# One core, two transformer blocks in fp32: chunk 0 of a chunked scan moved ahead of and between the steps of a pooling projection

## The chip, the core and the metric

The program runs on one core of a Trainium2 chip. The metric is the device time of one launch in microseconds (us), the median of three runs. Five engines work side by side and meet at semaphores: PE (TensorE, matmuls), DVE (VectorE), ACT (ScalarE), POOL (GpSimd), and SP (SyncE), which here only issues DMAs.

## What is computed

`reference()` runs two transformer blocks over 512 tokens of width 1024, batch 1. The change lies in the first block's hybrid mixer. Cut to that:

```python
proj = u @ w_in                                   # z, xbc, dt_raw, v
y = ssd_chunked(xs, dt, a, bm, cm)                # 4 chunks of 128 tokens, 16 heads of 64
y = y + d_skip[:, None] * xs
y = y.reshape(bsz, s, SSD_INNER) * silu(z)
y_ssd = rmsnorm(y, ssd_norm)
y_pool = multi_scale_pool(v, pool_w, pool_scale)  # 4 groups, a 256x256 product each, times pool_scale
return concatenate([y_ssd, y_pool]) @ w_out
```

Inside `ssd_chunked`, for a chunk c: `y_diag = (cb * seg) @ x`, where `seg = exp(a_cs[l] - a_cs[s])` below the diagonal; `states = b^T (decay * x)`; the running state is `prev[c+1] = exp(a_cs_end) * prev[c] + states[c]`; `y_off = (c @ prev[c]) * exp(a_cs)`. Chunk 0 has no `y_off`.

## The kernel before

Every fp32 product of this stretch is made of three matmuls over operands split into a high and a low part (`w_hi`/`w_lo`, `x_hi`/`x_lo`, `y_hi`/`y_lo`). Weights come in jobs of 256 columns: SP loads a job into `w_raw`, POOL splits it (`w_hi` in one instruction, `w_lo` in four) as soon as the job that last used the same half of `w_hi`/`w_lo` is through, which PE signals by `w_used`. PE writes job results into pairs of `g_bank`, everything small into the four `t_bank` banks, which are taken in turn by the position of a task in the table `TASKS`; PE waits on `t_free` of a bank until its last user has been read out. The order of instructions on each engine is written out by hand, one block per engine, and each engine works strictly in that order.

The stretch that the change touches follows the z projection. PE: `state(0)` (the state of chunk 0), the job `pool` (four groups of 12 matmuls, `products_T` with `kt=2`; two pairs of banks in turn, so group g waits for `yp_lo` of group g-2), `inside(0)` (y_diag of chunk 0, 32 small matmuls), then for each chunk c: `state(c)`, `from_state(c)` (y_off), `inside(c)`, and the job `wo_pool + c` of 48 matmuls, a quarter of the pooled half of the output projection. Between two of its 16 steps of three matmuls (`turned`), PE transposes the finished 128 tokens of the scan (task `yT{c}`, two banks).

A chunk's way over the other engines: DVE copies or adds the state (L2848, L2850), multiplies d_skip by xs (L2864), adds y_diag (L2869), multiplies by silu(z) (L2877, signals `y_ready`); ACT takes the sum of squares and the root (L2088, L2089); DVE prepares the next chunk's `xdt` (L2802) and state (L2886), takes the reciprocal (L2888, `yr_ready`); ACT scales `y_nat` (L1854, `yn_ready`); PE transposes (L1329); ACT writes `x_hi` from the banks (L1854) and DVE `x_lo` (L2899), which frees the banks. `decay(c)` on ACT turns the broadcast log decays of chunk c into `seg`: 16 instructions (L2058, "shifts", one per head) and one exponential (L2061, `seg_ready`); DVE multiplies them by the scores (L2814, `scores_decayed`, `m_ready`), in its order ahead of the x_lo of the chunk before. For the pooling ACT evicts `y_hi` (two instructions a group) and DVE `y_lo` (L2824).

The tasks of the table around chunk 0 stand in this order: state0, ydiag0, yT0, state1, yoff1, ydiag1, two banks each. SP sends the broadcast of chunk 2's decays (L651) once ydiag0 is done, and the weights of `wo_pool + 2` behind it. By the table yoff1 uses the two banks of yT0, and PE's `from_state(1)` waits until DVE has written the last `x_lo` of chunk 0. PE's own order is shown by `from_state`:

```python
pe.wait_ge(prev_ready, c)
for g in range(GROUPS):
    b = bank(TASKS[f"yoff{c}"] + g)      # waits for t_free of that bank
    nc.tensor.matmul(b, cT[...], state_into(c, g, g + 1), start=True, stop=True)
```

Of the kernel before, what the change touches and what calls it, by code (L numbers as in the profile page):

```python
# [231 lines left out]
def program(nc, A, out):  # L232
    with ExitStack() as ctx:
# [1618 lines left out]
        def _(act):  # L1852
# [224 lines left out]
            for g in range(4):  # L2077
                act.wait_ge(pool_group, g + 1)
                for f in range(2):
                    copy(y_hi[:, 2 * g + f, :], g_bank[:, 2 * ((j + 1 + g) % 2) + f, :], col["pool_scale"](2 * g + f)).then_inc(yp_hi, 1)  # L2080
            for c in range(CHUNKS):

                if c < CHUNKS - 1:
                    decay(c + 1)
# [534 lines left out]
        def _(dve):  # L2619
# [219 lines left out]
            for c in range(CHUNKS):  # L2839
                xv = xs_nat(c).rearrange("p (h d) -> p h d", h=HEADS)  # L2840
                halves = [slice(g * HPG, (g + 1) * HPG) for g in range(2)]
                if c < CHUNKS - 1:
                    for g in range(2):
                        r = TASKS[f"state{c}"] + g
                        b = ready(r).rearrange("p (k i d) -> p k i d", i=2, d=HD)
                        into = state_into(c + 1, g, g + 1)
                        if c == 0:
                            ins = v.tensor_copy(into, b)  # L2848
                        else:
                            ins = v.tensor_tensor(into, into, b, ALU.add)  # L2850
                        if g == 0:
                            ins.then_inc(t_free[BANK[r]], 1)
                        else:
                            done(ins, t_free[BANK[r]], prev_ready)
# [8 lines left out]

                link(v.tensor_tensor(xdd[:], xv, bc[:, 2, :].unsqueeze(2).to_broadcast([P, HEADS, HD]), ALU.mult))  # L2864
                for g in range(2):
                    r = TASKS[f"ydiag{c}"] + g
                    b = ready(r).rearrange("p (h d) -> p h d", h=HPG)
                    other = y_nat if c else xdd
                    ins = v.tensor_tensor(y_nat[:, halves[g], :], other[:, halves[g], :], b, ALU.add)  # L2869
                    if g == 0:  # L2870
                        ins.then_inc(t_free[BANK[r]], 1)
                    else:
                        done(ins, t_free[BANK[r]])
                if c:
                    link(v.tensor_tensor(y_nat[:], y_nat[:], xdd[:], ALU.add))
                dve.wait_ge(zs_ready, 4)
                v.tensor_tensor(y_nat[:], y_nat[:], zs[:, c, :].rearrange("p (h d) -> p h d", h=HEADS), ALU.mult).then_inc(y_ready, 1)  # L2877
# [668 lines left out]
```

## Time and profile before

| | |
|---|---|
| median of three runs | 1652.65 us (1652.22 to 1652.96) |
| the profiled execution | 1652.55 us, span 1650.8 us |
| PE busy | 1627.0 us, 99% of the span |
| DVE, ACT, POOL busy | 1046.3, 664.6, 1039.3 us |
| PE's granted clock, mean | 0.999 of full speed |

The span runs from the first to the last instruction of the profiled execution. The stretch that the change touches lies at 238 to 325 us of it.

### The profile page before, as it was taken

How to read it: one execution, taken by the hardware profiler on the slowest of the kernel's cores; microseconds unless marked ns; L12 is line 12 of the kernel's file. 1: busy time of each engine (PE TensorE's matmuls, PEld its weight loads, DVE VectorE, ACT ScalarE, POOL GpSimd, SP SyncE). 2: the span in 40 equal slices, each digit the busy share in tenths (PEclk: the TensorE clock that was granted, in tenths of full speed). 3: DMA queues.
4: the chain of work that ended last, by engine and by line, in shares of the span. 5: the costliest groups of instructions: out<-in, count | busy, mean ns of one | idle time of the engine just before them, and what ended most of it. 6: DMA issues, size and time to landing. Idle time of an engine off the chain costs nothing.

```text
span 1650.8 us, 23774 instructions
## 1 busy us (share of the span) xinstructions
PE 1627.0 (99%) x8755; PEld 1381.9 (84%) x8755; DVE 1046.3 (63%) x1634; ACT 664.6 (40%) x1166; POOL 1039.3 (63%) x788
## 2 busy tenths in 40 slices
PE   6999999999999999999999999999999999999998
PEld 5898897888978999999988888887878778877887
DVE  5323948773537745745757997999656786556624
ACT  5422237420324523623544446765312245555301
POOL 7676764566647784784765888784467643334664
PEclk9999999999999999999999999999999999999999
DMA  6333333322243242342334323222233222111231
GB/s 212 118 114 104 128 103 105 100 94 90 98 153 102 77 129 76 103 128 78 102 103 128 91 88 102 77 77 77 93 137 110 77 77 77 52 51 52 77 115 64
DMA packets 188347, 162.59 MB, mean 98 GB/s; under 512 B 7636, under 2 KB 184400, under 8 KB 187728
## 3 DMA queue, kind: packets, MB, share of 16 engines
q1 hardware_dynamic: 188040, 161.10, 30.7%
q8 instruction: 67, 1.10, 0.3%
q14 instruction: 40, 0.33, 0.1%
q10 hardware_dynamic: 200, 0.06, 0.0%
HBM read 155.87 MB, written 4.23 MB: 97 GB/s over the span
## 4 chain that ended last, share of the span: by engine, by line
PE 93%; DVE 4%; ACT 1%; DMA 1%; issue 1%; POOL 0%; DVEq 0%; SPq 0%; ACTq 0%
PE g_bank L1046 54%; PE g_bank L1420 10%; PE g_bank L1080 6%; PE g_bank L1070 5%; PE g_bank L1483 2%; PE t_bank L1420 2%; PE t_bank L1759 2%; PE g_bank L1629 1%; PE t_bank L1771 1%; PE t_bank L1371 1%; PE t_bank L1403 1%; PE t_bank L1748 1%; PE t_bank L1547 1%; PE t_bank L1568 1%; PE g_bank L1611 1%; PE t_bank L1304 1%
## 5 line engine op out<-in xcount | busy, mean ns | idle before, releaser
L803 POOL TENSOR_SCALAR w_hi<-w_raw 128x2048 fp32r<-128x2048 f32 x67 | 132.6, 1979 | 387.3 <-PE g_bank L1046 160.9
L820 POOL TENSOR_TENSOR w_lo<-w_raw,w_hi 128x512 fp32r<-128x512 f32 x264 | 367.0, 1421 | 5.5
L1046 PE MATMUL g_bank<-x_hi,w_hi 128*128 128x512 f32 x912 | 364.5, 400 | 0.4 <-DVEq L2633 0.4
L1046 PE MATMUL g_bank<-x_hi,w_lo 128*128 128x512 f32 x912 | 355.4, 390 | 0.0
L1046 PE MATMUL g_bank<-x_lo,w_hi 128*128 128x512 f32 x912 | 355.2, 389 | 0.0
L1046 PEld LDWEIGHTS g_bank<-x_hi,w_hi 128*128 128x128 f32 x912 | 171.3, 188 | 38.9 <-issue 4.8
L1046 PEld LDWEIGHTS g_bank<-x_hi,w_lo 128*128 128x128 f32 x912 | 171.2, 188 | 36.1
L1046 PEld LDWEIGHTS g_bank<-x_lo,w_hi 128*128 128x128 f32 x912 | 171.4, 188 | 35.2 <-issue 1.4
L3175 DVE SCALAR_TENSOR_TENSOR t_bank<-hc,cols,t_bank 128x512 f32<-128x512 f32 x280 | 187.0, 749 | 4.9 <-DVE hc L3159 3.0
L954 POOL TENSOR_TENSOR w_lo<-w_raw,w_hi 128x512 fp32r<-128x512 f32 x100 | 127.3, 1305 | 67.7 <-ACT w_hi L2279 67.7
L1046 PE MATMUL g_bank<-y_hi,w_hi 128*128 128x512 f32 x288 | 113.5, 394 | 0.0
L1046 PE MATMUL g_bank<-y_hi,w_lo 128*128 128x512 f32 x288 | 112.2, 390 | 0.0
L1046 PE MATMUL g_bank<-y_lo,w_hi 128*128 128x512 f32 x288 | 112.1, 389 | 0.0
L899 POOL TENSOR_TENSOR w_lo<-w_raw,w_hi 128x512 fp32r<-128x512 f32 x57 | 73.0, 1295 | 39.6 <-ACT w_hi L1854 39.6
L972 POOL TENSOR_TENSOR pacc<-pacc,prod 128x512 f32<-128x512 f32 x54 | 68.1, 1292 | 0.0
L1420 PE MATMUL g_bank<-x_lo,w_hi 128*128 128x256 f32 x228 | 64.5, 283 | 0.0
L1420 PE MATMUL g_bank<-x_hi,w_lo 128*128 128x256 f32 x228 | 64.5, 283 | 0.0
L1420 PE MATMUL g_bank<-xt_hi,w_hi 128*128 128x256 f32 x228 | 64.5, 283 | 0.0
L1420 PE MATMUL g_bank<-xt_lo,w_hi 128*128 128x256 f32 x228 | 64.5, 283 | 0.0
L1420 PE MATMUL g_bank<-xt_hi,w_lo 128*128 128x256 f32 x228 | 64.5, 283 | 0.0
L1420 PE MATMUL g_bank<-x_hi,w_hi 128*128 128x256 f32 x228 | 64.5, 283 | 0.0
L1046 PEld LDWEIGHTS g_bank<-y_hi,w_hi 128*128 128x128 f32 x288 | 54.1, 188 | 11.9 <-issue 0.7
(565 smaller groups left out, 3983.5 us busy)
## 6 DMA issues: line engine op xcount, KB each, us to landing
w_raw<-w_gate_up SPq DMA_DIRECT2D x44, 512.0 KB, 4.8
w_raw<-a_w_in SPq DMA_DIRECT2D x44, 512.0 KB, 4.4
w_raw<-b_w_in SPq DMA_DIRECT2D x38, 512.0 KB, 4.3
w_raw<-w_in SPq DMA_DIRECT2D x28, 512.0 KB, 4.5
w_raw<-w_kv SPq DMA_DIRECT2D x16, 512.0 KB, 4.3
w_raw<-w_out_mix SPq DMA_DIRECT2D x16, 512.0 KB, 6.3
w_raw<-w_down SPq DMA_DIRECT2D x16, 512.0 KB, 4.4
w_raw<-a_w_out SPq DMA_DIRECT2D x16, 512.0 KB, 4.3
```

The costliest lines, as they stand in the source:

```text
L803: nc.gpsimd.tensor_scalar(w_hi[:, par], w_raw[:, par], 1.0, 0.0, ALU.mult, ALU.add).then_inc(pool_chain, 1)
L820: last = nc.gpsimd.tensor_tensor(w_lo[:, par, s], w_raw[:, par, s], w_hi[:, par, s].bitcast(F32), ALU.subtract)
L899: return nc.gpsimd.tensor_tensor(lo, src, hi.bitcast(F32), ALU.subtract)
L954: last = nc.gpsimd.tensor_tensor(lo[:, s], w_raw[:, j % 2, s], hi[:, s].bitcast(F32), ALU.subtract)
L972: nc.gpsimd.tensor_tensor(acc_k[:], acc_k[:], p[:], ALU.add).then_inc(tap_chain, 1)
L1046: last = nc.tensor.matmul(g_bank[:, 2 * pair + f if banks is None else banks[f], 0:n], ww[:, k0 + k, ws], xk, start=(k == 0 and q == 0), s ...
L1070: last = nc.tensor.matmul(g_bank[:, 2 * par + f, :], ww[:, par, k, ws], xx[:, k0 + k, :], start=(k == 0 and q == 0), stop=(k == kt - 1 and ...
L1080: last = nc.tensor.matmul(g_bank[:, 2 * par + m // 2, m % 2 * WC:m % 2 * WC + n], xx[:, k, m * P:(m + 1) * P], ww[:, k, 0:n], start=(k == ...
L1420: last = nc.tensor.matmul(out, ww[:, k, :], xx[:, k, :], start=(k == 0 and q == 0), stop=(k == HK - 1 and q == 2))
L1483: last = nc.tensor.matmul(g_bank[:, DOWN_BANKS[c][0][f], :], ww[:, k, ws], xx[:, k, :], start=(k == 0 and q == 0), stop=(k == n - 1 and q ...
L1759: last = nc.tensor.matmul(b[:, c:c + W_OF[qb]], qB[:, 4 * hg + i, qb * P:(qb + 1) * P], kB[:, 0:W_OF[qb]], start=True, stop=True)
L3175: ins = v.scalar_tensor_tensor(tail if k == TAPS - 1 else a(k), h(k), wk, a(k), ALU.mult, ALU.add)
```

## The change

On PE, `inside(0)` is done right behind `state(0)`, ahead of the pooling's products. The last pooling group signals `w_used` itself, and the wait for all of `yp_lo` that stood between pooling and `wo_pool` is spread over steps 0, 6 and 7 of job `wo_pool`. The transposes of chunk 0 come after step 12 of that job and not after step 14. On DVE, the state, sums and d_skip product of chunk 0 stand ahead of the pooling's evictions, and the gate of chunk 0 between the second and the third of them. On ACT, the 16 shifts of chunk 1 are split: five behind the second pooling group, five behind the third, six with the exponential behind the scaling of chunk 0's `y_nat`, ahead of its `x_hi`. `add_state`, `add_inside` and `gated_by_z` are the old statements made into functions.

```diff
@@ -1306,6 +1306,7 @@
 
             j = JOBS["pool"]
             state(0)
+            inside(0)
             slot(j, j % 2, j // 2)
             for g in range(4):
                 if g == 0:
@@ -1314,12 +1315,12 @@
                     pe.wait_ge(yp_lo, 2 * g - 2)
                 pe.wait_ge(d_lo, 2 * g + 2)
                 last = products_T(j % 2, y_hi, y_lo, kt=2, k0=2 * g, x0=2 * g, pair=(j + 1 + g) % 2)
-                last.then_inc(pool_group, 1)
+                last.then_inc(pool_group if g < 3 else w_used, 1)
 
             def turned(c):
 
                 def turn(step):
-                    if step == (14 if c == 0 else 12):
+                    if step == 12:
                         pe.wait_ge(yn_ready, c + 1)
                         yv = y_nat[:].rearrange("p h d -> p (h d)")
                         for g in range(2):
@@ -1330,16 +1331,18 @@
                             last.then_inc(t_ready, 1)
                 return turn
 
-            inside(0)
-            pe.wait_ge(yp_lo, 8)
-            pe.nop().then_inc(w_used, 1)
+            def pool_rests(step):
+
+                if step in (0, 6, 7):
+                    pe.wait_ge(yp_lo, max(step, 5) + 1)
+
             for c in range(CHUNKS):
                 if c:
                     state(c)
                     from_state(c)
                     inside(c)
 
-                jobs(JOBS["wo_pool"] + c, 1, lambda par: products_T(par, y_hi, y_lo, between=turned(c)))
+                jobs(JOBS["wo_pool"] + c, 1, lambda par: products_T(par, y_hi, y_lo, between=turned(c), before=None if c else pool_rests))
             products_as_ready(JOBS["wo_ssd"], x_hi, x_lo, lambda k: pe.wait_ge(ys_lo, 8 * (CHUNKS - 1) + k + 1))
             pe.wait_ge(mem2_n, MT)
             for i in range(4):
@@ -2051,12 +2054,14 @@
             d_split(2)
             raw_pair(JOBS["v"] + 3)
 
-            def decay(c):
+            def decay(c, h0=0, h1=HEADS):
                 act.wait_ge(in_abc[c], 32)
-                for h in range(HEADS):
+                for h in range(h0, h1):
                     d = decay_of(c, h)
                     ins = nc.scalar.activation(d, d, ACT.Relu, bias=acs[:, c, h:h + 1], scale=-1.0)
                     ins.then_inc(relu_d, 1)
+                if h1 < HEADS:
+                    return
                 act.wait_ge(relu_d, HEADS * (c + 1))
                 nc.scalar.activation(decays(c), decays(c), ACT.Exp, scale=-1.0).then_inc(seg_ready, 1)
 
@@ -2075,12 +2080,17 @@
                 act.nop().then_inc(zs_ready, 1)
             j = JOBS["pool"]
             for g in range(4):
-                act.wait_ge(pool_group, g + 1)
+                if g < 3:
+                    act.wait_ge(pool_group, g + 1)
+                else:
+                    act.wait_ge(w_used, j + 1)
                 for f in range(2):
                     copy(y_hi[:, 2 * g + f, :], g_bank[:, 2 * ((j + 1 + g) % 2) + f, :], col["pool_scale"](2 * g + f)).then_inc(yp_hi, 1)
+                if g in (1, 2):
+                    decay(1, 5 * (g - 1), 5 * g)
             for c in range(CHUNKS):
 
-                if c < CHUNKS - 1:
+                if 0 < c < CHUNKS - 1:
                     decay(c + 1)
                 if c:
                     link(nc.scalar.activation(ysum[:, c, 1:2], eps[:, 0:1], ACT.Sqrt))
@@ -2089,6 +2099,8 @@
                 nc.scalar.activation(ysum[:, c, 1:2], ysum[:, c, 0:1], ACT.Sqrt, bias=eps[:, 0:1], scale=1.0 / SSD_INNER).then_inc(ysq_ready, 1)
                 act.wait_ge(yr_ready, c + 1)
                 copy(y_nat[:], y_nat[:], ysum[:, c, 0:1]).then_inc(yn_ready, 1)
+                if c == 0:
+                    decay(1, 10)
                 for g in range(2):
                     b = ready(TASKS[f"yT{c}"] + g)
...
+            def add_state(c):
+
+                for g in range(2):
+                    r = TASKS[f"state{c}"] + g
...
@@ -2873,8 +2862,48 @@
                         done(ins, t_free[BANK[r]])
                 if c:
                     link(v.tensor_tensor(y_nat[:], y_nat[:], xdd[:], ALU.add))
+
+            def gated_by_z(c):
+
                 dve.wait_ge(zs_ready, 4)
                 v.tensor_tensor(y_nat[:], y_nat[:], zs[:, c, :].rearrange("p (h d) -> p h d", h=HEADS), ALU.mult).then_inc(y_ready, 1)
+
+            add_state(0)
+            add_inside(0)
+            j = JOBS["pool"]
+            for k in range(8):
+
+                if k == 2:
+                    gated_by_z(0)
+                dve.wait_ge(yp_hi, k + 1)
+                ins = v.scalar_tensor_tensor(y_lo[:, k, :], g_bank[:, 2 * ((j + 1 + k // 2) % 2) + k % 2, :], col["pool_scale"](k),
+                                             y_hi[:, k, :].bitcast(F32), ALU.mult, ALU.subtract)
+                done(ins, yp_lo, *([g_free[j % 2]] * (k == 7)))
+            def add_projection(c):
+
+                j = JOBS["wo_pool"] + c
+                dve.wait_ge(w_used, j + 1)
+                for f in range(2):
+                    k = 2 * c + f
+                    ins = v.tensor_tensor(hT[:, k, :], hT[:, k, :], g_bank[:, 2 * (j % 2) + f, :], ALU.add)
+                    if f == 0:
...
```

PE from `state(0)` to the transposes of chunk 0, before (L1286 is state, L1046 the jobs' products, L1304 y_diag, L1329 the transposes; the names behind "waits" are the semaphores; "..." stands for more rows of L1046):

```order
L1286 MATMUL t_bank<-xdd,b_nat 128x512 [waits t_free2,xdt_ready]
L1286 MATMUL t_bank<-xdd,b_nat 128x512 [waits t_free3]
L1046 MATMUL g_bank<-y_hi,w_hi 128x512 [waits g_free0,d_lo,g_free1,w_split]
...
L1046 MATMUL g_bank<-y_hi,w_hi 128x512 [waits d_lo,yp_lo]
...
L1304 MATMUL t_bank<-xdt,m__99 128x64 [waits t_free0,m_ready]
L1304 MATMUL t_bank<-xdt,m__99 128x64 x7
L1304 MATMUL t_bank<-xdt,m__99 128x64 [waits t_free1]
L1304 MATMUL t_bank<-xdt,m__99 128x64 x7
L1046 MATMUL g_bank<-y_hi,w_hi 128x512 [waits yp_lo,g_free0,w_split]
...
L1329 MATMUL t_bank<-ident,y_nat 128x128 [waits t_free2,yn_ready]
```

and in the changed kernel (the transposes are L1330 there):

```order
L1286 MATMUL t_bank<-xdd,b_nat 128x512 [waits t_free2,xdt_ready]
L1286 MATMUL t_bank<-xdd,b_nat 128x512 [waits t_free3]
L1304 MATMUL t_bank<-xdt,m__99 128x64 [waits t_free0,m_ready]
L1304 MATMUL t_bank<-xdt,m__99 128x64 x7
L1304 MATMUL t_bank<-xdt,m__99 128x64 [waits t_free1]
L1304 MATMUL t_bank<-xdt,m__99 128x64 x7
L1046 MATMUL g_bank<-y_hi,w_hi 128x512 [waits g_free0,d_lo,g_free1,w_split]
...
L1046 MATMUL g_bank<-y_hi,w_hi 128x512 [waits d_lo,yp_lo]
...
L1046 MATMUL g_bank<-y_hi,w_hi 128x512 [waits yp_lo,g_free0,w_split]
...
L1046 MATMUL g_bank<-y_hi,w_hi 128x512 [waits yp_lo]
...
L1046 MATMUL g_bank<-y_hi,w_hi 128x512 [waits yp_lo]
...
L1330 MATMUL t_bank<-ident,y_nat 128x128 [waits t_free2,yn_ready]
```

y_diag of chunk 0 has moved up past the 48 matmuls of the pooling, three waits for `yp_lo` stand inside the job behind it, and the transposes stand two steps earlier in that job.

ACT from the second pooling group to the first `x_hi` of chunk 0, before (`m_xl` holds the decays of chunk 1, L1854 is a copy):

```order
L1854 ACTIVATE y_hi<-g_bank,cols 128x512 [waits pool_group]
L1854 ACTIVATE y_hi<-g_bank,cols 128x512
L2058 ACTIVATE m_xl<-m_xl,acs 128x128 [waits in_abc1]
L2058 ACTIVATE m_xl<-m_xl,acs 128x128 x15
L2061 ACT_TABLE_LOAD
L2061 ACTIVATE m_xl<-m_xl 128x8x256 [waits relu_d]
L2088 ACTIVATE xdd,ysum<-y_nat 128x1024 [waits y_ready]
L2089 ACT_TABLE_LOAD
L2089 ACTIVATE ysum<-ysum,eps 128x1 [waits act_chain]
L1854 ACTIVATE y_nat<-y_nat,ysum 128x1024 [waits yr_ready]
L1854 ACTIVATE x_hi<-t_bank,cols 128x128 [waits t_ready]
```

and in the changed kernel (L1857 is the copy, L2061 the shifts, L2066 the exponential):

```order
L2061 ACTIVATE m_xl<-m_xl,acs 128x128 [waits in_abc1]
L2061 ACTIVATE m_xl<-m_xl,acs 128x128 x4
...
L2061 ACTIVATE m_xl<-m_xl,acs 128x128 [waits in_abc1]
L2061 ACTIVATE m_xl<-m_xl,acs 128x128 x4
...
L2099 ACTIVATE ysum<-ysum,eps 128x1 [waits act_chain]
L1857 ACTIVATE y_nat<-y_nat,ysum 128x1024 [waits yr_ready]
L2061 ACTIVATE m_xl<-m_xl,acs 128x128 [waits in_abc1]
L2061 ACTIVATE m_xl<-m_xl,acs 128x128 x5
L2066 ACT_TABLE_LOAD
L2066 ACTIVATE m_xl<-m_xl 128x8x256 [waits relu_d]
L1857 ACTIVATE x_hi<-t_bank,cols 128x128 [waits t_ready]
```

The shifts of chunk 1 are split in three, and the last six of them, a table load and the exponential now stand between the scaling of `y_nat` and the first `x_hi`.

## Rows read from the trace of the kernel before

**Rows 1.** Page, part 1: busy us, share of the span, instructions.

```profile
PE 1627.0 (99%) x8755; PEld 1381.9 (84%) x8755; DVE 1046.3 (63%) x1634; ACT 664.6 (40%) x1166; POOL 1039.3 (63%) x788
```

**Rows 2.** Waits of PE, 220 to 330 us: total, times, longest.

```profile
PE t_bank L1329 <- ACT y_nat L1854: 1.3, 1, 1.3
```

**Rows 3.** Timeline of PE, chunk 0: start, duration, instruction, count [idle before].

```profile
240.40 0.53 PE L1046 MATMUL g_bank<-y_hi,w_hi 128*128 128x512 f32 x1
...
251.59 3.68 PE L1304 MATMUL t_bank<-xdt,m__99 128*128 128x64 f32 x32
255.07 0.48 PE L1046 MATMUL g_bank<-y_hi,w_hi 128*128 128x512 f32 x1
...
266.87 1.09 PE L1329 MATMUL t_bank<-ident,y_nat 128*128 128x128 f32 x8 [1.30 <-ACT y_nat L1854]
...
268.49 1.88 PE L1286 MATMUL t_bank<-xdd,b_nat 128*128 128x512 f32 x4
...
271.70 0.70 PE L1294 MATMUL t_bank<-prev,cT 128*128 128x512 f32 x1 [0.25 <-DVEq L2633]
```

**Rows 4.** Timeline of PE, chunk 1 and the start of chunk 2.

```profile
272.66 3.68 PE L1304 MATMUL t_bank<-xdt,m_xl 128*128 128x64 f32 x32
276.15 0.48 PE L1046 MATMUL g_bank<-y_hi,w_hi 128*128 128x512 f32 x1
...
285.10 1.03 PE L1329 MATMUL t_bank<-ident,y_nat 128*128 128x128 f32 x8
...
288.05 1.88 PE L1286 MATMUL t_bank<-xdd,b_nat 128*128 128x512 f32 x4
289.76 1.88 PE L1294 MATMUL t_bank<-prev_x,cT 128*128 128x512 f32 x4
```

**Rows 5.** Timeline of DVE, pooling to the end of chunk 0.

```profile
244.22 0.75 DVE L2824 SCALAR_TENSOR_TENSOR y_lo<-g_bank,cols,y_hi 128x512 fp32r<-128x512 f32 x1 [18.23 <-ACT y_hi L1854]
...
252.50 1.65 DVE L2824 SCALAR_TENSOR_TENSOR y_lo<-g_bank,cols,y_hi 128x512 fp32r<-128x512 f32 x2 [1.07 <-ACT y_hi L1854]
...
260.88 2.32 DVE L2802 TENSOR_TENSOR xdt<-xs,dt__105 128x1024 f32<-128x1024 f32 x1
263.12 2.31 DVE L2886 TENSOR_TENSOR prev_x<-prev,cdec 128x1024 f32<-128x1024 f32 x1
...
266.67 2.35 DVE L2814 TENSOR_TENSOR m_xl<-m_xl,cbm 128x1024 f32<-128x1024 f32 x2
...
270.37 1.12 DVE L2899 SCALAR_TENSOR_TENSOR x_lo<-t_bank,cols,x_hi 128x128 fp32r<-128x128 f32 x4 [0.31 <-PE t_bank L1286]
```

**Rows 6.** Instructions on tile y_nat, the gate's: ns min/median/max, starts.

```profile
L2877 DVE TENSOR_TENSOR y_nat<-y_nat,zs x4: 1226/1226/2021, 258.9 to 316.3; 128x1024 f32<-128x1024 f32 x4
```

**Rows 7.** Timeline of ACT, chunk 0.

```profile
251.78 1.26 ACT L1854 ACTIVATE y_hi<-g_bank,cols 128x512 fp32r<-128x512 f32 x2 [1.45 <-PE g_bank L1046]
...
265.66 1.15 ACT L1854 ACTIVATE y_nat<-y_nat,ysum 128x1024 f32<-128x1024 f32 x1 [1.91 <-DVE ysum L2888]
...
269.57 4.80 ACT L2058 ACTIVATE m__99<-m__99,acs 128x128 f32<-128x128 f32 x16
274.39 1.28 ACT L2061 ACT_TABLE_LOAD   x1
275.68 1.92 ACT L2061 ACTIVATE m__99<-m__99 128x2048 f32<-128x2048 f32 x1
```

**Rows 8.** Timeline of POOL, the splits of two weight tiles.

```profile
254.49 1.91 POOL L803 TENSOR_SCALAR w_hi<-w_raw 128x2048 fp32r<-128x2048 f32 x1 [8.29 <-PEq L1335]
256.48 7.86 POOL L820 TENSOR_TENSOR w_lo<-w_raw,w_hi 128x512 fp32r<-128x512 f32 x4
268.85 1.92 POOL L803 TENSOR_SCALAR w_hi<-w_raw 128x2048 fp32r<-128x2048 f32 x1 [4.51 <-PE g_bank L1046]
```

**Rows 9.** Timeline of PE at the start, behind an idle stretch.

```profile
12.79 3.67 PE L1139 MATMUL t_bank<-ident,xn_nat 128*128 128x128 f32 x16 [2.35 <-ACT xn_nat L1854]
```

**Rows 10.** The same stretch by windows: busy us (instructions) of each engine, PE's granted clock.

```profile
12.79:16.46 3.67, 3.67 (x17) 3.67 (x18) 1.38 (x2) 2.16 (x4) 3.50 (x5) 1.00 1.05 382
```

More of the change, by code:

```diff
@@ L2819, in _, with add_inside @@
             scores_decayed(0)
+            def add_state(c):
+                for g in range(2):
+                    r = TASKS[f"state{c}"] + g
+                    b = ready(r).rearrange("p (k i d) -> p k i d", i=2, d=HD)
+                    into = state_into(c + 1, g, g + 1)
+                    if c == 0:
+                        ins = v.tensor_copy(into, b)
+                    else:
+                        ins = v.tensor_tensor(into, into, b, ALU.add)
+                    if g == 0:
+                        ins.then_inc(t_free[BANK[r]], 1)
+                    else:
+                        done(ins, t_free[BANK[r]], prev_ready)
+            halves = [slice(g * HPG, (g + 1) * HPG) for g in range(2)]
+            def add_inside(c):
+                xv = xs_nat(c).rearrange("p (h d) -> p h d", h=HEADS)
+                link(v.tensor_tensor(xdd[:], xv, bc[:, 2, :].unsqueeze(2).to_broadcast([P, HEADS, HD]), ALU.mult))
+                for g in range(2):
+                    r = TASKS[f"ydiag{c}"] + g
+                    b = ready(r).rearrange("p (h d) -> p h d", h=HPG)
+                    other = y_nat if c else xdd
+                    ins = v.tensor_tensor(y_nat[:, halves[g], :], other[:, halves[g], :], b, ALU.add)
+                    if g == 0:
+                        ins.then_inc(t_free[BANK[r]], 1)
+                    else:
+                        done(ins, t_free[BANK[r]])
+                if c:
+                    link(v.tensor_tensor(y_nat[:], y_nat[:], xdd[:], ALU.add))
+            def gated_by_z(c):
+                dve.wait_ge(zs_ready, 4)
+                v.tensor_tensor(y_nat[:], y_nat[:], zs[:, c, :].rearrange("p (h d) -> p h d", h=HEADS), ALU.mult).then_inc(y_ready, 1)
+            add_state(0)
+            add_inside(0)
             j = JOBS["pool"]
             for k in range(8):
+                if k == 2:
+                    gated_by_z(0)
                 dve.wait_ge(yp_hi, k + 1)
@@ L2839, in _ @@
             for c in range(CHUNKS):
[L2840 to L2854, printed above, removed]
+                if 0 < c < CHUNKS - 1:
+                    add_state(c)
                 if c:
@@ L2862, in _ @@
                                         ALU.mult).then_inc(t_free[BANK[r]], 1)
[L2864 to L2877, printed above, removed]
+                    add_inside(c)
+                    gated_by_z(c)
                 if c < CHUNKS - 1:
```

## Prediction, before the changed kernel was run

> **What bounds the kernel now.** The page comes first: PE is busy for 99% of the span [rows 1], so nearly everything added to PE's path lengthens the run, and nothing can be gained but PE's waits. The view of waits, narrowed to the stretch of the change, says how much that is: one wait of 1.3 us, for ACT's scaling of y_nat ahead of the transposes of chunk 0 [rows 2]. PE's timeline shows the second, smaller one: the second y_off of chunk 1 starts at 271.70 behind an idle 0.25 us, released by DVE [rows 3]; in chunk 2 the state and y_off follow each other 1.71 us apart, with no wait [rows 4]. The reader should then look at the other engines' timelines not for busy shares but for what ends when: DVE finishes the last x_lo of chunk 0 at 271.49 [rows 5], and PE goes on 0.21 us later [rows 3]. That pair of banks is the joint between the chunks. All times below are of the profiled execution (1652.55 us, its span 1650.8); it lies 0.1 us under the median of the runs, so a difference found in it is simply added to the median.
>
> **y_diag ahead of the pooling.** The 32 small matmuls take 3.48 us before (251.59 to 255.07) and the four pooling groups 11.19 us (240.40 to 251.59), 2.80 us each [rows 3]. Exchanged, y_diag runs from 240.40 to 243.9, and the groups end at 246.7, 249.5, 252.3 and 255.1. Their sum is the same, so this costs nothing by itself. The work that DVE gains before the first eviction lies in 18.2 us in which it is idle today [rows 5]. The gate does not: it lands between the second and the third eviction. The first eviction starts 1.0 us behind its group's end (244.22 against 240.40 + 2.80), a pair takes 1.65 us [rows 5], and the gate takes 1.23 us where nothing disturbs it, 2.02 us where POOL splits beside it [rows 6]. Four evictions and the gate end at 246.7 + 1.0 + 1.65 + 0.2 + 1.23 + 1.65 = 252.4 us; the fourth group needs them at 252.3. That is a new wait of 0.15 us (0.9 us at 2.02). I take 0.15, since POOL's earlier split should be through by then. Job wo_pool 0 starts at 255.25 instead of 255.07. On SP the broadcast of chunk 2's decays waits for y_diag of chunk 0, and a weight load stands behind it; both can now go some 11 us earlier (255.07 to 243.9), and since nobody waits for them sooner, and POOL still splits by `w_used`, this is nothing either way. The waits at its steps 0, 6 and 7 ask for evictions that trail each group by as much as today, 2.56 us behind the last (254.15 against 251.59) [rows 3, 5], and step 6 is over 4 us into the job: nothing.
>
> **Shifts among the evictions.** Sixteen take 4.80 us, 0.30 each [rows 7]. ACT's eviction of a group ends 1.45 us behind the group (253.04 against 251.59), five shifts take 1.5 us, in all 2.95 us, against 2.80 + 0.20 us to the next eviction: they just fit. Cost nothing, at most 0.1.
>
> **Transposes at step 12.** In chunk 1 they come 8.95 us into the job (276.15 to 285.10) [rows 4], so PE wants them at 264.2. DVE ends its last eviction at 255.25 + 2.56 = 257.8, starts xdt 0.24 later, needs 4.55 us for xdt and the state (260.88 to 265.43), and 1.44 us later PE can go on (266.87) [rows 3, 5]: 264.0. In time. The whole job then takes the 11.90 us of chunk 1 (276.15 to 288.05) [rows 4] and ends at 267.15, 1.34 us before today's 268.49. This is the gain that the change can hold, up to here.
>
> **What now stands ahead of x_hi.** ACT ends the scaling at 264.0, and then come six shifts (1.8), the table load (1.28) and the exponential (1.92) [rows 7]: 269.0. Before, all of this lay ahead of the y_ready of chunk 0, in a stretch in which ACT had nothing else to do. Two things queue behind it: x_hi on ACT, and on DVE, which goes in order, the scores of chunk 1, and behind these x_lo, which frees the banks of yT0. PE is done with state 1 at 267.15 + 1.71 = 268.85 [rows 4] and stands before y_off.
>
> The scores took 2.35 us undisturbed (266.67 to 269.02), ahead of POOL's next split [rows 5, 8]. Now they meet it. POOL starts 0.36 us behind the end of the job (268.85 against 268.49) [rows 3, 8], so at 267.5, and its first instruction runs for 1.9 us, to 269.4. What such a meeting costs is shown by xdt and the state: 2.3 us each under the split of 256.48 against 1.2 us for a score instruction of the same size [rows 5, 8]; that is, they take turns, 1.15 us each. So: first scores from 269.4 to 270.6, POOL to 271.75, second scores to 272.9. From there to the last x_lo it is 2.47 us as before (269.02 to 271.49), x_hi being written beside the scores: 275.35, and PE's second y_off at 275.55 (+0.21) instead of 271.70. Behind it, order and durations are those of before on every engine, PE has no wait there that could swallow the delay, and DVE's chain for chunk 1 is delayed by the same amount. **Sum: +3.85 us**, 1656.5 us. All gains of the part before (1.34 us) are in it.
>
> What the notes say of such a load would make it worse. Before the exponential the load takes 1.28 us, and the exponential starts within 0.02 us of its end (274.39 + 1.28 against 275.68) [rows 7]. The Trainium skill (ScalarE: Activation LUTs, What ACT_TABLE_LOAD costs) puts a drain of about 1.38 us beside each load, 2.66 us in all. By that the scores would start at about 270.4 and the sum be about +5; the trace shows no such drain, and the sum goes by the trace.
>
> **The rivals.**
> A, the forecast: +3.85. Its own spread is the waits sized above, the order in which DVE and POOL meet, and a turn lost or won (1.15): 1655.7 to 1657.6.
> B, PE loses its rate as well. It would stand idle from about 269.2 to 274.05 (x_lo of the first bank, 272.9 + 1.12 + a hand-over), far longer than any wait before [rows 2]. The only stretch behind an idle time of this length is the program's start: there 16 transposes take 3.67 us, against 1.03 us for eight in chunk 1 [rows 4, 9], 1.6 us more, though the granted clock reads 1.00, which is 2.4 GHz [rows 10]. For it: the slow start. Against it: that clock column, and that the first transposes may have waited for ACT. Price: 1.6 to 2.5 us on top of A, 1658.1 to 1659.0. The Trainium skill (TensorE: Matmul & The Clock Gate, Why this matters for your kernels) says that a TensorE left idle between bursts of matmuls falls to half clock, which speaks for B; these rows neither show such a fall nor exclude it.
> C, DVE and POOL do not take turns over the scores (they hit POOL's first instruction, which is of another kind than those of 256.48): 269.05 + 2.35 + 2.47 + 0.21 = 274.1, +2.4, 1655.0. Not distinguishable from before.
> D, not slower: the split of 255.6 does not hold up xdt and the state, so each takes 1.2 instead of 2.3 us. y_nat is scaled 2.2 us earlier, the exponential ends at 266.8, before POOL starts, the scores end at 269.15 and y_off comes at 271.85: +0.15, 1652.8. It decides from the point where the scores end before 272.3 us (then the delay is under 3.3 us). Against it: this split begins at the end of the pooling today as well, and xdt and the state lie under it [rows 5, 8].
>
> **How the numbers follow.** 0.2% is 3.3 us, about what a measurement of this kernel tells from no change. A has 0.50, B 0.30, C 0.14, D 0.06. Most of A (0.42) and all of B lie over 1655.95: slower 0.72. The rest of A, C and most of D are within 0.2%: 0.26. Faster would take more than 3.3 us of gain where PE's waits hold about 2 us: 0.02. The range takes in A, C and nearly all of B, 1654.8 to 1658.9; A alone is 1655.7 to 1657.6.
>
> **What the profile of the changed kernel would show.** Right: no idle time of PE ahead of the transposes of chunk 0; state 1 at about 267.2; then PE idle for about 5 us ahead of the first y_off of chunk 1, put down to DVE, and 0.6 us ahead of the second; the exponential of chunk 1 at about 267; the two score instructions together near 3.8 us; y_diag of chunk 1 at about 276.5 instead of 272.66. For B: matmul durations doubled behind the wait, or a granted clock of 0.5. Wrong: x_hi written before the exponential (then I misread ACT's order), a wait at the third or fourth pooling group of over a microsecond, or a wait later in the kernel that shrinks by as much as this one grows.

## The result, and the profile after

The changed kernel takes 1659.81 us (median of five runs, 1657.61 to 1662.10), against 1652.65 us (1651.52 to 1652.96) before: a ratio of 1.0047, 95% interval 1.0036 to 1.0058, 7.2 us longer. The prediction had 1656.5 us and a range up to 1658.9. One of the five executions, at 1657.61 us, lies within that range; its mean granted clock is 0.998, that of the others 0.994 or 0.995. Of the experiments below, e3 and e4 had one execution each at a mean clock of 0.85 and 0.57 (1806 and 2674 us), which is left out of every figure here.

The profiled execution took 1660.07 us, its span is 1658.4 us. Everything up to the state of chunk 0 is the same program in both kernels, yet it starts at 237.02 us here and at 238.82 us in the profile of before; over the profiles of this study it varies from 236.8 to 239.0 us. So I give places as times behind that start, S, in what follows. The view of waits of PE, 235 to 330 us, has one line:

```profile
PE t_bank L1294 <- DVEq L2645: 5.0, 1, 5.0
```

The 1.3 us of [rows 2] are gone, and 5.0 us ahead of the first y_off of chunk 1 have come, more than there was to win. PE's timeline:

```profile
237.02 1.88 PE L1286 MATMUL t_bank<-xdd,b_nat 128*128 128x512 f32 x4
...
250.69 0.50 PE L1046 MATMUL g_bank<-y_hi,w_hi 128*128 128x512 f32 x1
...
262.41 1.03 PE L1330 MATMUL t_bank<-ident,y_nat 128*128 128x128 f32 x8
...
265.34 1.88 PE L1286 MATMUL t_bank<-xdd,b_nat 128*128 128x512 f32 x4
272.20 3.75 PE L1294 MATMUL t_bank<-prev,cT 128*128 128x512 f32 x4 [4.99 <-DVEq L2645]
275.75 6.93 PE L1304 MATMUL t_bank<-xdt,m_xl 128*128 128x64 f32 x32
282.44 0.77 PE L1046 MATMUL g_bank<-y_hi,w_hi 128*128 128x512 f32 x1
283.01 0.63 PE L1046 MATMUL g_bank<-y_lo,w_hi 128*128 128x512 f32 x1
...
295.65 1.88 PE L1286 MATMUL t_bank<-xdd,b_nat 128*128 128x512 f32 x4
```

Against [rows 3, 4]: the transposes come at S+25.39 without a wait, the state of chunk 1 at S+28.32 instead of S+29.67, y_off at S+35.18. But look at the durations behind the wait: y_diag, 32 matmuls, takes 6.93 us and not 3.68, and the first products of the next job start 0.43 us apart, not 0.23. From y_diag on (S+38.73 instead of S+33.84, +4.89) the delay grows to +8.09 at the start of job wo_pool 1 (282.44, S+45.42 instead of S+37.33) and +9.40 at the state of chunk 2 (S+58.63 instead of S+49.23). The windows say why (busy us of PE, PEld, DVE, ACT, POOL with their instructions, granted clock, share of the DMA engines, GB/s):

```profile
268.00:270.00 2.00, 0.00 (x0) 0.00 (x0) 2.00 (x2) 2.00 (x9) 2.00 (x2) 1.00 0.00 0
270.00:272.00 2.00, 0.00 (x0) 0.00 (x0) 1.91 (x5) 2.00 (x9) 2.00 (x2) 0.88 0.00 0
272.00:274.00 2.00, 1.80 (x2) 0.79 (x3) 1.54 (x5) 1.97 (x7) 2.00 (x2) 0.50 0.00 0
278.00:280.00 2.00, 2.00 (x11) 2.00 (x11) 1.76 (x2) 0.00 (x0) 0.00 (x0) 0.50 0.03 8
284.00:286.00 2.00, 2.00 (x8) 1.57 (x7) 1.97 (x3) 0.00 (x0) 0.00 (x0) 0.71 0.00 0
```

The granted clock falls to 0.50, 1.2 GHz, late in PE's idle stretch (0.88 over 270 to 272 is full clock up to about 271.5) and is back at 1.00, 2.4 GHz, at about 285.2 (0.71 over 284 to 286): 13.6 us at half clock. Such times of a fall are worked out from the share of a window that was spent at each of the two levels. The 9.4 us of this stretch, less the 1.8 us by which this execution reached it sooner, are the 7.6 us between the spans.

DVE, ACT and POOL in the same stretch, one view each:

```profile
247.79 1.22 DVE L2869 TENSOR_TENSOR y_nat<-y_nat,zs 128x1024 f32<-128x1024 f32 x1
...
256.36 1.92 DVE L2814 TENSOR_TENSOR xdt<-xs,dt__105 128x1024 f32<-128x1024 f32 x1 [0.24 <-DVE y_lo L2879]
258.19 2.31 DVE L2915 TENSOR_TENSOR prev_x<-prev,cdec 128x1024 f32<-128x1024 f32 x1
...
266.90 3.97 DVE L2826 TENSOR_TENSOR m_xl<-m_xl,cbm 128x1024 f32<-128x1024 f32 x2 [4.17 <-ACT m_xl L2066]
...
272.22 1.12 DVE L2928 SCALAR_TENSOR_TENSOR x_lo<-t_bank,cols,x_hi 128x128 fp32r<-128x128 f32 x4 [0.31 <-DVE x_lo L2928]
```

```profile
260.73 1.15 ACT L1857 ACTIVATE y_nat<-y_nat,ysum 128x1024 f32<-128x1024 f32 x1 [3.08 <-DVE ysum L2917]
261.79 1.85 ACT L2061 ACTIVATE m_xl<-m_xl,acs 128x128 f32<-128x128 f32 x6
263.66 1.28 ACT L2066 ACT_TABLE_LOAD   x1
264.95 1.91 ACT L2066 ACTIVATE m_xl<-m_xl 128x2048 f32<-128x2048 f32 x1
266.77 2.15 ACT L1857 ACTIVATE x_hi<-t_bank,cols 128x128 fp32r<-128x128 f32 x8
```

```profile
265.70 1.90 POOL L803 TENSOR_SCALAR w_hi<-w_raw 128x2048 fp32r<-128x2048 f32 x1 [1.82 <-PE g_bank L1046]
267.68 6.78 POOL L820 TENSOR_TENSOR w_lo<-w_raw,w_hi 128x512 fp32r<-128x512 f32 x4
```

ACT has the scaling of y_nat done at 261.9, and only at 266.8 begins with x_hi; the exponential lies between. DVE waits 4.17 us for it, then takes 3.97 us for the two score instructions, which took 2.35 us [rows 5], because POOL's split lies beside them, and the last x_lo ends at 273.34.

### The profile page after: what moved, and what is told of

It is laid out like the page before. It is cut to its first block, busy times and chain, and to the rows that moved or that the text cites. A ratio compares the mean times of both kernels' runs of the same rounds, so it can differ in the third digit from the quotient of the medians.

```text
span 1658.4 us, 23772 instructions
## 1 busy us (share of the span) xinstructions
PE 1632.3 (98%) x8755; PEld 1386.9 (84%) x8755; DVE 1047.3 (63%) x1634; ACT 663.0 (40%) x1165; POOL 1041.2 (63%) x788
## 4 chain that ended last, share of the span: by engine, by line
PE 93%; DVE 4%; ACT 2%; issue 1%; DMA 1%; POOL 0%; DVEq 0%; SPq 0%; ACTq 0%
PE g_bank L1046 53%; PE g_bank L1423 10%; PE g_bank L1080 6%; PE g_bank L1070 5%; PE g_bank L1486 2%; PE t_bank L1423 2%; PE t_bank L1762 2%; PE g_bank L1632 1%; PE t_bank L1774 1%; PE t_bank L1304 1%; PE t_bank L1374 1%; PE t_bank L1406 1%; PE t_bank L1751 1%; PE t_bank L1550 1%; PE t_bank L1571 1%; PE g_bank L1220 1%
## 5 line engine op out<-in xcount | busy, mean ns | idle before, releaser
L1046 PE MATMUL g_bank<-x_hi,w_hi 128*128 128x512 f32 x912 | 364.5, 400 | 0.3 <-DVEq L2645 0.2
L1046 PE MATMUL g_bank<-x_hi,w_lo 128*128 128x512 f32 x912 | 355.4, 390 | 0.0
L1046 PE MATMUL g_bank<-x_lo,w_hi 128*128 128x512 f32 x912 | 355.2, 390 | 0.0
L1046 PEld LDWEIGHTS g_bank<-x_hi,w_hi 128*128 128x128 f32 x912 | 171.3, 188 | 38.7 <-issue 4.8
L1046 PEld LDWEIGHTS g_bank<-x_hi,w_lo 128*128 128x128 f32 x912 | 171.2, 188 | 36.2
L1046 PEld LDWEIGHTS g_bank<-x_lo,w_hi 128*128 128x128 f32 x912 | 171.5, 188 | 35.1 <-issue 1.4
L1046 PE MATMUL g_bank<-y_hi,w_hi 128*128 128x512 f32 x288 | 114.0, 396 | 0.0
L1046 PE MATMUL g_bank<-y_hi,w_lo 128*128 128x512 f32 x288 | 112.7, 391 | 0.0
L1046 PE MATMUL g_bank<-y_lo,w_hi 128*128 128x512 f32 x288 | 112.6, 391 | 0.0
L1046 PEld LDWEIGHTS g_bank<-y_hi,w_hi 128*128 128x128 f32 x288 | 54.5, 189 | 11.8 <-DVEq L2645 0.6
```

What stands on the lines that cost most here:

```text
L1046: last = nc.tensor.matmul(g_bank[:, 2 * pair + f if banks is None else banks[f], 0:n], ww[:, k0 + k, ws], xk, start=(k == 0 and q == 0), s ...
```

## The experiments

Nine kernels were run. Six change only the order of instructions, and three (e1, e5, e6) add matmuls; the places that they are compared by are the starts of y_off and y_diag of chunk 1 behind S. From the added matmuls nothing is computed: they go into a bank pair that the next job overwrites.

### e1: PE works through its wait

```diff
 state(c)
+if c == 1:
+    n1 = JOBS["wo_pool"] + 1
+    slot(n1, n1 % 2, n1 // 2)
+    for i in range(20):
+        nc.tensor.matmul(g_bank[:, 2 * (n1 % 2), :], w_hi[:, n1 % 2, i % 8, 0:P], y_hi[:, i % 8, :], start=True, stop=True)
 from_state(c)
```

> The changed kernel with 20 matmuls of 128x512 put between the state of chunk 1 and its y_off, into a bank pair that the next job overwrites, so that PE works through its 5.0 us wait instead of standing idle; nothing is computed from them. Theory (the wait alone costs about 3.8 us, the rest of the loss is PE's clock falling behind the idle stretch): the clock stays at 1.00, y_off still starts at the same place (some 35.2 us behind the state of chunk 0), y_diag and the job behind it run at full rate, and the time is about 1656.3 us, 3.7 over before. Rival (the clock falls for another reason, such as the small matmuls of y_diag moved ahead, or the loss lies in a later stage): the time stays near 1660 us, and the clock reads 0.5 as well.

1655.56 us (nine runs, 1655.19 to 1656.91), ratio 1.0023 (1.0013 to 1.0033), on the chip where before took 1652.34. PE's timeline and one window:

```profile
268.46 5.15 PE L1346 MATMUL g_bank<-y_hi,w_hi 128*128 128x512 f32 x20
274.04 1.10 PE L1294 MATMUL t_bank<-prev,cT 128*128 128x512 f32 x2 [0.44 <-DVEq L2650]
275.39 1.12 PE L1294 MATMUL t_bank<-prev,cT 128*128 128x512 f32 x2 [0.25 <-DVEq L2650]
276.35 3.68 PE L1304 MATMUL t_bank<-xdt,m_xl 128*128 128x64 f32 x32
```

```profile
272.00:274.00 2.00, 1.60 (x8) 0.98 (x6) 1.75 (x5) 2.00 (x8) 2.00 (x2) 1.00 0.00 0
```

y_off starts at S+35.22 (S is 238.82), where it did (S+35.18); the clock is 1.00 throughout, y_diag takes 3.68 us, and starts at S+37.53, 3.69 us later than before. The span is 3.8 us longer than that of before with the same S. So the wait costs 3.7 us, and the fall of the clock the other 5.7 of the 9.4 us of the profiled execution. The medians give less to the clock: 3.2 us over before with the added matmuls, 7.2 without them. The executions of the changed kernel differ in it: in the one with a mean clock of 0.998 the clock was down for less time, if at all (its trace is not kept). The rival, that the clock falls for the small matmuls moved ahead of the pooling, is out: they are still there.

### e2: the exponential ahead of the scaling

```diff
+if c == 0:
+    decay(1, 10)
 act.wait_ge(yr_ready, c + 1)
 copy(y_nat[:], y_nat[:], ysum[:, c, 0:1]).then_inc(yn_ready, 1)
-if c == 0:
-    decay(1, 10)
...
-if step == 12:
+if step == (14 if c == 0 else 12):
```

> The changed kernel with the last six shifts and the exponential of chunk 1 ahead of ACT's scaling of y_nat, in the 3.1 us in which ACT waits for DVE's reciprocal, and the transposes of chunk 0 back at step 14. Theory (the loss comes from the exponential standing ahead of x_hi, and the scores and x_lo behind it): scores start 4.1 us earlier, before POOL's next split, y_off of chunk 1 waits for under 1.5 us, the clock stays at 1.00, y_diag of chunk 1 starts about 32.8 us behind the state of chunk 0 (33.8 before), and the time is about 1651.6 us, 1.0 under before. Rival (the order of the shifts is not it): near 1660 us, with the wait of 5 us still ahead of y_off or ahead of the transposes.

1650.84 us (ten runs, 1649.43 to 1651.76), ratio 0.9992 (0.9982 to 1.0002). DVE and PE:

```profile
263.81 3.46 DVE L2826 TENSOR_TENSOR m_xl<-m_xl,cbm 128x1024 f32<-128x1024 f32 x2
...
268.62 1.13 DVE L2928 SCALAR_TENSOR_TENSOR x_lo<-t_bank,cols,x_hi 128x128 fp32r<-128x128 f32 x4 [0.31 <-PE t_bank L1286]
```

```profile
268.60 1.10 PE L1294 MATMUL t_bank<-prev,cT 128*128 128x512 f32 x2 [0.21 <-DVEq L2645]
...
270.91 3.68 PE L1304 MATMUL t_bank<-xdt,m_xl 128*128 128x64 f32 x32
```

All 9.4 us are gone, and y_diag starts at S+32.76 (S is 238.15), 1.08 us sooner than before. With the six shifts, the load and the exponential in the 3 us in which ACT waits for the reciprocal anyway, they hold up nothing but the scaling, by 1.8 us (S+25.54 instead of S+23.71), which step 14 allows. Against before the interval touches 1.0002, so that the gain of 1.5 us is not clear of the noise by the medians; y_diag 1.08 us sooner speaks for it. The place of the exponential is the cause of the loss; the return to step 14 is not what heals it, since e9 keeps step 12 and has no loss either.

### e3: the shifts in one piece, as before

```diff
-if g in (1, 2):
-    decay(1, 5 * (g - 1), 5 * g)
...
-if 0 < c < CHUNKS - 1:
+if c < CHUNKS - 1:
     decay(c + 1)
...
-if c == 0:
-    decay(1, 10)
```

> The changed kernel with ACT's shifts and exponential of chunk 1 in one piece behind the pooling, as before; PE and DVE as changed. Theory: ACT reaches the sum of squares 8 us later, the transposes of chunk 0 wait for about 5 us, y_off of chunk 1 for about 0.9; without a fall of the clock 2.9 us over before (1655.6), with one 1658 to 1661. Rival (the split of the shifts alone makes the loss, and moving y_diag and the gate is harmless): no wait over 2 us, 1651 to 1653 us.

1656.78 us (eight runs, 1655.50 to 1657.51), ratio 1.0029 (1.0018 to 1.0039). The transposes and two windows:

```profile
266.90 1.97 PE L1330 MATMUL t_bank<-ident,y_nat 128*128 128x128 f32 x8 [4.50 <-ACT y_nat L1857]
```

```profile
264.00:266.00 2.00, 0.00 (x0) 0.00 (x0) 0.50 (x2) 1.68 (x3) 0.00 (x0) 0.59 0.00 0
...
270.00:272.00 2.00, 2.00 (x8) 1.60 (x7) 1.55 (x6) 2.00 (x8) 0.00 (x0) 0.71 0.00 0
```

The wait of 4.5 us has moved to the transposes of chunk 0 (5 expected), and there was none left ahead of y_off (0.9 expected, which was wrong). The clock fell here too, at about 264.4, but it was back at about 271.2, 4.3 us behind the restart; the time lies between the 1655.6 expected without a fall and the 1658 to 1661 with one. So the changes on PE and DVE make a loss even without the split on ACT. The transposes at step 12 have a part in it: two steps are 1.4 us, so at step 14 the wait would be some 3.1 us (an estimate, not run), still more than the 1.3 of before. With y_diag early, ACT's work on the decays is what the norm of chunk 0 waits for. Splitting it was needed; where its last part went was not.

### e4: POOL's split kept away from the scores

```diff
 broadcast_decays(2)
+sp.wait_ge(m_ready, 2)
 stream(JOBS["wo_pool"] + 2, 1, w_cols("w_out_mix", 2 * WC, 8))
```

> The changed kernel with SP holding the load of the weights of job wo_pool 2 until the scores of chunk 1 are done, so that POOL's split of them cannot lie beside the scores; the split is needed only some 30 us later. Theory (DVE and POOL take turns over the two score instructions, 3.97 us against 2.35): the scores take 2.35 us, PE's idle time ahead of y_off shrinks from 5.0 to 3.4 us, y_diag of chunk 1 starts 35.9 us behind the state of chunk 0; with the clock up 1654.7 us, if it falls nonetheless 1658 to 1660. Rival (POOL is not what slows the scores): scores still 3.9 us, idle time 5.0 us, 1660 us.

1660.06 us (four runs, 1658.85 to 1660.37), ratio 1.0047 (1.0031 to 1.0063). DVE; PE; one window:

```profile
267.55 2.36 DVE L2827 TENSOR_TENSOR m_xl<-m_xl,cbm 128x1024 f32<-128x1024 f32 x2 [4.16 <-ACT m_xl L2067]
```

```profile
271.24 1.10 PE L1295 MATMUL t_bank<-prev,cT 128*128 128x512 f32 x2 [3.37 <-DVEq L2646]
...
274.46 6.93 PE L1305 MATMUL t_bank<-xdt,m_xl 128*128 128x64 f32 x32
```

```profile
272.00:274.00 2.00, 1.75 (x3) 0.84 (x3) 1.67 (x4) 2.00 (x8) 0.00 (x0) 0.57 1.08 381
```

The scores take 2.36 us, and the first y_off comes at S+33.59 (S is 237.65), 1.6 us sooner than in the changed kernel: the collision with POOL is shown, at 1.6 us. Of this, 1.0 us is left at the state of chunk 2 (S+57.65 instead of S+58.63), and nothing in the medians, since an idle time of 3.4 us brought the clock down as well, and y_diag again took 6.93 us. The fall came at about 272.3, 1.0 us after PE had gone on: two matmuls of y_off took 1.10 us, the next two 2.08.

### e5: a shorter idle time

Against e1:

```diff
-for i in range(20):
+for i in range(9):
```

> The changed kernel with 9 instead of 20 matmuls of 128x512 between the state of chunk 1 and its y_off (nothing is computed from them), so that PE stands idle for about 3.0 us instead of 5.0. It asks how short an idle time still brings the clock down; 1.3 us before the change did not, 3.4 us with the split held back did. If it stays up: as with 20 matmuls, 1655.6 us. If it falls: y_diag and the first products of the next job at half rate as in the changed kernel, 1659 to 1660 us.

Five runs: 1655.64, 1656.31, 1657.53, 1660.92 and 1661.20 us, with mean granted clocks of 0.999, 0.998, 0.998, 0.994 and 0.994; ratio 1.0041 (1.0028 to 1.0055). The profiled one is the first:

```profile
273.58 1.10 PE L1294 MATMUL t_bank<-prev,cT 128*128 128x512 f32 x2 [2.92 <-DVEq L2650]
...
275.89 3.68 PE L1304 MATMUL t_bank<-xdt,m_xl 128*128 128x64 f32 x32
```

Neither outcome but both: with 2.9 us of idle time the profiled execution kept its clock (no window of this stretch reads under 1.00), and two others, 5 us longer, have the mean clock of the changed kernel's fall. The two at 0.998 can be either: e8's profiled execution has this mean with the clock at 1.00 in the whole stretch.

### e6: wide matmuls first, behind the wait

Against e1, the added matmuls behind the wait instead of ahead of it:

```diff
 state(c)
+from_state(c)
 if c == 1:
 ...
-    for i in range(20):
+    for i in range(16):
 ...
-from_state(c)
 inside(c)
```

> The changed kernel with 16 matmuls of 128x512 behind the wait, between y_off of chunk 1 and its y_diag (nothing is computed from them); 3.6 us of work at full rate. Theory (the clock stays down as long as it does, 13 us, because the narrow matmuls of y_diag, 128x64, come first; with ACT's shifts in one piece 512-column work followed the wait and the clock was back 4 to 5 us behind it): the clock is back at 1.00 within 5 to 7 us of the first y_off, y_diag takes 3.5 us instead of 6.7, and the time is 1659.5 to 1661, no more than 1.2 over the changed kernel despite the added work. Rival (the clock stays down for a fixed time of some 13 us, whatever runs): the added matmuls run at half rate too, y_diag takes 6.7 us, and the time is 1664 us or more.

1661.42 us (four runs, 1661.28 to 1662.31), ratio 1.0056 (1.0041 to 1.0072). PE and two windows:

```profile
282.41 3.68 PE L1304 MATMUL t_bank<-xdt,m_xl 128*128 128x64 f32 x32
```

```profile
278.00:280.00 2.00, 2.00 (x6) 1.58 (x5) 1.69 (x4) 0.85 (x2) 0.00 (x0) 0.50 0.00 0
280.00:282.00 2.00, 2.00 (x10) 1.61 (x10) 0.98 (x1) 0.00 (x0) 0.00 (x0) 0.98 0.03 8
```

The clock is back at about 280.1, 6.0 us behind the first y_off instead of 13.0, and y_diag runs in 3.68 us. A fixed time of some 13 us, the rival, is out. 16 more matmuls, 3.6 us at full rate, cost 1.6 us by the medians (0.4 above what was expected). At the state of chunk 2 the delay is 9.79 us (S+59.02): 3.69 of wait, 3.6 of added work, and only 2.5 of clock, where the changed kernel has 5.7.

### e7: x_hi and x_lo first

```diff
 # ACT: x_hi of chunk 0, then
+if c == 0:
+    decay(1, 10)
...
 # DVE: x_lo of chunk 0, then
+if c == 0:
+    scores_decayed(1)
```

Each is taken out of its place ahead of them.

> The changed kernel with chunk 0's x_hi ahead of the last six shifts and the exponential on ACT, and chunk 0's x_lo ahead of the scores of chunk 1 on DVE. Theory: the banks are free in time and y_off of chunk 1 does not wait (it starts some 30.1 us behind the state of chunk 0), but the scores end at about 37 us behind it, so PE waits about 5 us ahead of y_diag instead; the clock falls again; 1658 to 1661 us. Rival (only the order of x_hi and the exponential makes the loss): no wait over 1.5 us, 1651 to 1652 us.

1660.88 us (four runs, 1659.79 to 1661.25), ratio 1.0054 (1.0039 to 1.0069). Waits of PE, 20 to 340 us, and DVE:

```profile
PE t_bank L1304 <- DVE prev_x L2842: 6.5, 1, 6.5
```

```profile
270.03 4.49 DVE L2826 TENSOR_TENSOR m_xl<-m_xl,cbm 128x1024 f32<-128x1024 f32 x2 [3.35 <-ACT m_xl L2066]
```

y_off does not wait (266.87, S+30.06), and y_diag waits 6.5 us (5 expected) for the scores, which now take 4.49 us for two, 3.4 of them beside POOL's split (it ends at 273.44). The order of x_hi and the exponential alone is not the cause: the next chunk needs both, and in the versions without a loss (e2, e9) the exponential is done before the transposes.

### e8: also POOL's split away from chunk 0

On top of e2: the shifts four behind the first pooling group, five, five and two, the transposes at step 12, and on SP

```diff
-stream(JOBS["wo_pool"] + 1, 1, w_cols("w_out_mix", WC, 8))
 sp.wait_ge(t_ready, TASKS["ydiag0"] + 2)
 broadcast_decays(2)
+sp.wait_ge(ysq_ready, 1)
+stream(JOBS["wo_pool"] + 1, 1, w_cols("w_out_mix", WC, 8))
```

> The changed kernel with the exponential of chunk 1 ahead of the scaling of y_nat, the shifts of chunk 1 as four behind the first pooling group, five, five and two, the transposes at step 12, and the load of wo_pool 1 held until chunk 0's root is taken, so that POOL's split of it does not lie beside DVE's xdt, state and scores. Theory: xdt and the state take 1.2 us each instead of 1.9 and 2.3, the scores start 24.5 us behind the state of chunk 0 (25.7 in the version with the exponential early) and take about 2.4 us instead of 3.5, the second y_off starts about 30.3 us behind it (31.8), no wait of PE over 0.9 us: 1649.3 to 1650.0 us. Rival (the load comes too late and PE waits for the split ahead of job wo_pool 1, or DMAs collide): over 1651 us.

1655.21 us (eleven runs, 1653.51 to 1655.53), ratio 1.0016 (1.0007 to 1.0025), slower than before. PE; DVE; POOL:

```profile
286.11 1.09 PE L1331 MATMUL t_bank<-ident,y_nat 128*128 128x128 f32 x8 [2.56 <-ACT y_nat L1858]
```

```profile
258.29 1.22 DVE L2815 TENSOR_TENSOR xdt<-xs,dt__105 128x1024 f32<-128x1024 f32 x1 [0.24 <-DVE y_lo L2880]
...
263.43 2.36 DVE L2827 TENSOR_TENSOR m_xl<-m_xl,cbm 128x1024 f32<-128x1024 f32 x2 [1.46 <-ACT m_xl L2067]
...
279.11 2.20 DVE L2870 TENSOR_TENSOR y_nat<-y_nat,zs 128x1024 f32<-128x1024 f32 x1
```

```profile
274.60 7.87 POOL L821 TENSOR_TENSOR w_lo<-w_raw,w_hi 128x512 fp32r<-128x512 f32 x4
```

Chunk 0 went as expected (xdt in 1.22 us, scores in 2.36 from S+24.5, y_diag at S+31.98). But the two splits held back now lie beside DVE's sums and gate of chunk 1 (the gate in 2.20 us against 1.23), and PE waits 2.6 us for the transposes of chunk 1. Neither theory had that; the 1649.3 to 1650.0 us expected were missed by 5 us. The profiled run is the fastest of the eleven, five lie at 1653.5 to 1654.1 and six at 1655.2 to 1655.5; what divides them was not profiled.

### e9: e8 without the load held back

Against the changed kernel, all of it on ACT:

```diff
-if g in (1, 2):
-    decay(1, 5 * (g - 1), 5 * g)
+if g < 3:
+    decay(1, (0, 4, 9)[g], (4, 9, 14)[g])
...
+if c == 0:
+    decay(1, 14)
 act.wait_ge(yr_ready, c + 1)
 copy(y_nat[:], y_nat[:], ysum[:, c, 0:1]).then_inc(yn_ready, 1)
-if c == 0:
-    decay(1, 10)
```

> As the version with the exponential early (1650.8 us), with the shifts of chunk 1 as four behind the first pooling group, five, five and two, and the transposes at step 12; no load is held. Theory: ACT scales y_nat 1.2 us earlier, but the joint between the chunks is then set by DVE's scores, which lie beside POOL's split and end where they did (29.1 us behind the state of chunk 0), so the second y_off stays at 31.8 us: 1650.5 to 1651.0 us, faster than before by about 0.1%. Rival (ACT's scaling sets the joint): 1649.6 us.

1651.26 us (eleven runs, 1649.74 to 1651.89) beside 1652.58, ratio 0.9993 (0.9984 to 1.0002). DVE and PE:

```profile
264.63 3.43 DVE L2826 TENSOR_TENSOR m_xl<-m_xl,cbm 128x1024 f32<-128x1024 f32 x2
```

```profile
271.71 3.68 PE L1304 MATMUL t_bank<-xdt,m_xl 128*128 128x64 f32 x32
```

y_nat is scaled 1.15 us sooner than in e2 (S+24.39 against S+25.54), and y_diag starts at the same S+32.75. The joint is set by DVE's scores beside POOL, as the theory had it; the rival is out. The time is 0.3 us over the range expected, and as in e2, the 1.3 us against before are not clear of the noise.

## Why the prediction was wrong, point by point

**What bounds the kernel: right.** Nothing behind the scan swallowed the delay: from S to the end of the span it is 1421.4 us against 1412.0 before, the same 9.4 us that stand at the state of chunk 2.

**y_diag ahead of the pooling: right.** The fourth pooling group was forecast at S+13.63 (252.45) and came at S+13.67, and DVE's gate took the 1.22 us that were assumed.

**Shifts among the evictions, transposes at step 12: right.** Transposes forecast at S+25.38, measured S+25.39; the state of chunk 1 at S+28.33, measured S+28.32.

**What now stands ahead of x_hi: right in mechanism and size.** The first y_off was forecast at S+35.23 and came at S+35.18; the scores, forecast at 3.8 us, took 3.97; y_diag was forecast at S+37.7, and came at S+37.53 in e1, where the clock stays up. The sum of +3.85 us for the wait was 3.7. One detail was off: the scores did not wait for the end of POOL's first instruction, as forecast, but started at S+29.88, 0.7 us sooner than the S+30.58 of the sum, and took longer, so that they ended within 0.3 us of the forecast. e4 shows the turn-taking with POOL that C denied (2.36 against 3.97 us); e2 shows that the place of the exponential is the cause. The drain that the Trainium skill (ScalarE: Activation LUTs, What ACT_TABLE_LOAD costs) puts beside a load does not show: the load of 1.28 us from 263.66 starts 0.02 us behind the last shift and is followed by the exponential at 264.95.

**The step that failed is the clock: the forecast's sum, A, put it at nothing, and rival B, which had it, was wrong in its chance and in its price.** I gave it 0.30, holding against it a clock column that read 1.00 at the program's start and transposes that may have waited for ACT. Both arguments were weak, and the trace of before shows it. The transposes at the start took 421 ns each at the median, not 273 as later, and waiting for ACT stands in the rows as idle time, not in the duration of an instruction. And the end of the same trace, which the prediction leaves out, has a fall in the clock column (windows, as above):

```profile
1646.00:1648.00 2.00, 0.00 (x0) 0.00 (x0) 1.93 (x4) 0.00 (x0) 0.74 (x1) 1.00 0.55 207
1648.00:1650.00 2.00, 0.00 (x0) 0.00 (x0) 0.38 (x1) 0.00 (x0) 0.00 (x0) 0.58 0.85 316
```

PE's last matmul ends at 1643.9, and at about 1648.3, after 4.4 us of idleness, the clock goes to 0.50; the forecast had 5 us of idleness. In the runs the fall took place in every profile with an idle stretch of 3.4 us or more (the changed kernel, e3, e4, e6, e7). And I priced it at 1.6 to 2.5 us from the only slow stretch that the trace had, the first 16 transposes, as if a fall had one price. It costs what PE does while the clock is down: 13.6 us of y_diag and products here, 5.7 us, against 2.5 us in e6, where the clock is back after 6.8 us. What the price depended on was not in the rows that I took it from. With 5.7 in place of 1.6 to 2.5 the sum of the forecast gives 9.6 us, and the stretch of the profiled execution shows 9.4. By the medians the clock costs 3.9 us (7.16 less the 3.22 of e1), which is over B's price too.

The Trainium skill (TensorE: Matmul & The Clock Gate, Why this matters for your kernels) had the rule that decided the case, that a TensorE idle between bursts falls to half clock; the trace of the changed kernel agrees, with 0.50 behind an idle time of 5.0 us.

**Direction and D: right, and out.** Slower by more than 3.3 us; xdt and the state took 1.92 and 2.31 us beside POOL's split.

## What to carry to other kernels

A wait on the busiest engine has two prices: its length, which the chain of releases gives to within some tenths of a microsecond, and, if it is long enough for the clock to fall, the half rate of all that follows until the clock is back, which can be the larger one. Before work is put between two steps of another engine, ask what queues behind it on every engine: here one exponential, moved past a copy, held x_hi, behind it x_lo, behind it two banks, and so the whole of PE. A gap in which the engine waits anyway (ACT's for the reciprocal) is the place for it.

## What the runs showed of the hardware

The same program with an idle stretch of 2.9 us kept its TensorE clock in the profiled execution and, by the mean clocks, lost it in two others (e5, means of 0.999 and 0.994, 1655.6 and 1661.2 us). In e8's profile 2.6 us of idleness left the clock at 1.00. Nor does the fall come at a fixed distance behind PE's last matmul: it was 2.0 us in e3, 2.2 in e7, 4.2 in e6, 4.3 in the changed kernel and 4.4 in e4. How long the clock stays down differs with what comes next: 13.6 us where y_off and 32 matmuls of 64 columns come first, 6.8 us where 512-column matmuls follow y_off (e6, full clock up to about 273.2, back at 280.1), and as long, 6.8 us, with transposes and 512-column products behind the wait (e3). In e4 and e7, where the 32 narrow matmuls also came ahead of the next job, it was 13.7 us. Whether the narrow matmuls are the reason or only their place in time was not separated further.

A VectorE instruction with two SBUF inputs of 128x1024 takes 1.22 us alone and 1.9 to 2.3 beside POOL's split (xdt 1.22 in e8 and 1.92 in the changed kernel; two scores 2.36 in e4, 3.97 in the changed kernel and 4.49 in e7), as if the two took turns. The x_lo, which have one input in PSUM, lose nothing: four x_lo take 1.12 us beside the split (272.22 in the changed kernel) and the four of chunk 1 at 294.57, with POOL idle, 1.13.
